# Attention head: the wait for the score banks behind seven projection steps, four steps after the first scores, three steps beside the first eleven units

## The chip, the core and the metric

The kernel runs on one core of a Trainium2 chip. The core has TensorE (matmuls, PE in the profile, its weight loads PEld), VectorE (DVE), ScalarE (ACT), GpSimd (POOL) and SyncE (SP, which issues DMAs only). The metric is device time in microseconds. TensorE writes its results to PSUM, which has eight banks of 128 x 512 floats; the other engines work on SBUF, and VectorE and ScalarE also read PSUM.

## What is computed

Two transformer blocks follow each other on 512 tokens of width 1024. The second has two layers, each with an attention, and the change lies in these two attentions. Cut to them:

```python
for layer in range(2):
    xn = rmsnorm(h, norm_mix[layer])
    if layer == 0:   # causal attention with a forget bias
        q, k, v, f_logit, qm = split(xn @ w_in_fox)
        mix = fox_attention(q, k, v, log_sigmoid(f_logit + b_forget))
    else:            # rotary positions, three dilated branches in one softmax by a mask
        q, k, v, qm = split(xn @ w_in_dil)
        mix = dilated_attention(apply_rope(q), apply_rope(k), v)
    mem_out = memory_attention(qm, rmsnorm(mem), w_mem_kv[layer])   # 256 memory tokens
    h = h + merge_heads(concat(mix, mem_out)) @ w_out[layer]        # 12 + 4 heads of 64
    h = h + conv_ffn(rmsnorm(h, norm_ffn[layer]), ...)
```

## The kernel before

Everything is float32. A projection tile ("piece") is 128 output columns by 512 tokens: eight blocks of 128 input features, each with three matmuls (high by high, high by low, low by high part), so 24 matmuls of 512 columns. `product_steps` (L1662) yields after every two blocks, so that a piece is four **steps** of six matmuls. GpSimd loads the weight pieces two ahead into four slots: the high part by DMA, its negation (L497), and the low part by an adding DMA (L500); it starts a piece when TensorE begins the one three places ahead of it.

`attention(layer, ready)` (L1799) works through 32 **units**: eight pairs of heads (two memory pairs, then six mixing pairs) by four blocks of 128 queries. The keys of a unit are 256 wide for a memory pair and 128, 256, 384, 512 for the blocks of a mixing pair. The projections q0, k0, v0, q1 ... v5 (`BESIDE_PIECES`, 18 pieces, 72 steps) run beside the units, and after them 14 short steps of the output projection (`head_block`, three matmuls each): 86 steps in all. TensorE's order is written out by hand: two steps, scores(0), four steps, and then for each unit u: scores(u+1), one step, possibly the transposes of a v piece, the transposes of unit u's probabilities (`turned`), the rest of `steps_of(u)`, and the output of unit u-1.

Between them the other engines do the softmax of a unit: VectorE adds the bias or mask and takes the maximum (`top_of`, L925, L927), ScalarE takes the exponents (L1602), VectorE divides (`divided`, L933, L935), TensorE transposes, ScalarE copies the transposed probabilities out of banks 4 and 5 (`kept`, L1610).

Banks: scores use 2 and 3, the beside pieces alternate between 0 and 1, and the pieces ahead of them (in layer 0 the forget piece, then memq0 and memq1) use 6, 7 and 2. Who empties a beside piece's bank: in layer 0 VectorE, for q and k with L862 and for v with L877; in layer 1 ScalarE for q and k (`rope_copy`, L1364), VectorE for v. In layer 1 a q or k piece is then rotated: SP moves its four strips into the shared tile `work[:, 4]` (four transfers, L475), and `rotated` on VectorE (L869 to L871) ends with the count `taken`. SP waits for the `taken` of one piece before it moves the next.

`done_at()` counts the steps and says in which unit a piece is complete (`DONE_AT`); from it all engines take when they evict (one unit later), take a v piece (two later) or rotate (three later).

```python
                for at in (2, 3):
                    pe.wait_ge(S(freed[at][0]), freed[at][1])
                if layer:
                    pe.wait_ge(S("mask_in"), 16)
                steps = beside()
                for _ in range(FIRST_STEPS[0]):
                    next(steps)
                scores(0)
```

Of the kernel before, what the change touches and what calls it, by code (L numbers as in the profile page):

```python
# [139 lines left out]
BESIDE_PIECES = [f"{name}{pair}" for pair in range(NP) for name in "qkv"]  # L140
FIRST_STEPS = (2, 4)


def steps_of(u):

    return 3 if u < 11 or u % 4 == 1 else 2

# [47 lines left out]
def build(nc, A, out):  # L195
# [17 lines left out]
    with ExitStack() as ctx:  # L213
# [303 lines left out]
        def _(dve):  # L517
# [321 lines left out]
            def vector_layer(layer):  # L839
# [97 lines left out]
                def beside(u):  # L937
# [3 lines left out]
                    for name, at in zip(BESIDE_PIECES, DONE_AT):  # L941
                        if u == at + taken_after(name, layer):
                            if name[0] == "v":
                                value_taken(name)
                            elif layer:
                                rotated(name)
                    for name, at in zip(BESIDE_PIECES, DONE_AT):
                        if u == at + 1:
                            if name[0] == "v":
# [5 lines left out]

                top_of(0)
                divided(0)
                for u in range(len(UNITS) + 2):
# [321 lines left out]
        def _(act):  # L1280
# [16 lines left out]
            def skip(tiles):  # L1297
                n.next("tile", tiles)
                n.value["bank"] += tiles
# [271 lines left out]
            for layer in range(2):  # L1571
# [33 lines left out]
                def kept(u):  # L1605
# [4 lines left out]
                    do(act.activation(at_m["pt"][:, u % 2, :, 0:width], banks8[:, 4:6, 0:width], ACT.Copy), "probs_kept")  # L1610

                exponents(0)
                for u in range(len(UNITS) + 2):
                    if u >= QB + 1 and (u - 1) % QB == 0:
                        pair_high(PAIRS[(u - 1) // QB - 1])
                    if u + 1 < len(UNITS):
                        exponents(u + 1)
                    for name, at in zip(BESIDE_PIECES, DONE_AT):
                        if u == at + 1:
                            if name[0] == "v" or layer == 0:  # L1620
                                skip(1)
                            else:
                                rope_copy(name)
                    if u < len(UNITS):
# [22 lines left out]
        def _(pe):  # L1647
# [151 lines left out]
            def attention(layer, ready):  # L1799
# [86 lines left out]
                def output(u):  # L1886
# [12 lines left out]
                    mm.then_inc(S("head_out"), 1)  # L1899

                for at in (2, 3):
                    pe.wait_ge(S(freed[at][0]), freed[at][1])
                if layer:
                    pe.wait_ge(S("mask_in"), 16)
                steps = beside()
                for _ in range(FIRST_STEPS[0]):
                    next(steps)
                scores(0)
# [402 lines left out]
```

## Time and profile before

| | us |
|---|---|
| median of three runs | 2222.05 |
| lowest and highest | 2220.85, 2223.23 |
| the profiled execution's own time | 2216.38 |
| its span in the trace | 2214.6 |
| TensorE busy in the span | 2099.2 (95%) |
| VectorE, GpSimd, ScalarE busy | 1290.1, 844.8, 466.4 |

The attention of layer 0 lies between about 983 and 1186 us, that of layer 1 between about 1597 and 1800 us. In the rows of a timeline a matmul's duration is modelled and overlaps the next one; the distance between the starts is its real cost in a stream. A bracket at the end of a row tells how long the engine sat idle before it and what released it.

### The profile page before, as it was taken

How to read it: one execution, taken by the hardware profiler on the slowest of the kernel's cores; microseconds unless marked ns; L12 is line 12 of the kernel's file. 1: busy time of each engine (PE TensorE's matmuls, PEld its weight loads, DVE VectorE, ACT ScalarE, POOL GpSimd, SP SyncE). 2: the span in 40 equal slices, each digit the busy share in tenths (PEclk: the TensorE clock that was granted, in tenths of full speed). 3: DMA queues.
4: the chain of work that ended last, by engine and by line, in shares of the span. 5: the costliest groups of instructions: out<-in, count | busy, mean ns of one | idle time of the engine just before them, and what ended most of it. 6: DMA issues, size and time to landing. Idle time of an engine off the chain costs nothing.

```text
span 2214.6 us, 27273 instructions
## 1 busy us (share of the span) xinstructions
PE 2099.2 (95%) x10722; PEld 1669.6 (75%) x10722; DVE 1290.1 (58%) x1798; ACT 466.4 (21%) x852; POOL 844.8 (38%) x1008
## 2 busy tenths in 40 slices
PE   6999898998899999989999999999899999999996
PEld 4778786676788888867777888888676678888885
DVE  7686664448662342574565763727546757637274
ACT  3013301213210000123333210202233432102011
POOL 1333323233444444433222444444422324444442
PEclk7999999999999999999999999999999999999998
DMA  8978776589998988866665889898776648899885
GB/s 285 206 176 190 146 144 143 115 222 244 247 237 187 194 194 196 191 147 153 128 138 132 189 181 203 192 193 181 173 152 133 131 110 188 189 198 193 193 188 123
DMA packets 124615, 394.40 MB, mean 178 GB/s; under 512 B 26028, under 2 KB 28076, under 8 KB 124232
## 3 DMA queue, kind: packets, MB, share of 16 engines
q0 software_dynamic: 96480, 346.20, 72.5%
q1 hardware_dynamic: 28008, 46.45, 6.6%
q8 instruction: 85, 1.39, 0.3%
q14 instruction: 42, 0.34, 0.0%
HBM read 385.63 MB, written 3.94 MB: 176 GB/s over the span
## 4 chain that ended last, share of the span: by engine, by line
PE 76%; DVE 13%; DMA 7%; issue 1%; ACT 1%; SPq 1%; POOL 1%; DVEq 0%; ACTq 0%
PE ps L1674 65%; DMA w_lo<-in_w 4%; PE ps L1703 2%; PE ps L1870 2%; PE ps L1897 1%; PE ps L1883 1%; DMA arena<-in_ada 1%; DMA w_hi<-in_w 1%; DVE work L754 1%; PE ps L2062 1%; DVE small L927 1%; DVE arena L755 1%; DVE arena L637 1%; DVE arena L925 1%; POOL w_lo L497 1%
## 5 line engine op out<-in xcount | busy, mean ns | idle before, releaser
L1674 PE MATMUL ps<-h_hi,w_hi 128*128 128x512 f32 x1760 | 710.9, 404 | 36.6 <-DVE arena L862 14.4
L1674 PE MATMUL ps<-h_lo,w_hi 128*128 128x512 f32 x1760 | 690.7, 392 | 0.0
L1674 PE MATMUL ps<-h_hi,w_lo 128*128 128x512 f32 x1760 | 690.6, 392 | 0.0
L491 POOL DMA_DIRECT2D w_hi<-in_w x334 | 186.6, 559 | 1166.8 <-PE ps L1674 1032.3
L1674 PEld LDWEIGHTS ps<-h_hi,w_hi 128*128 128x128 f32 x1760 | 333.4, 189 | 129.3 <-issue 25.1
L1674 PEld LDWEIGHTS ps<-h_hi,w_lo 128*128 128x128 f32 x1760 | 333.1, 189 | 71.6
L497 POOL TENSOR_SCALAR w_lo<-w_hi 128x1024 fp32r<-128x1024 f32 (+1 forms) x334 | 360.0, 1078 | 69.5 <-DMA w_hi<-in_w 64.0
L1674 PEld LDWEIGHTS ps<-h_lo,w_hi 128*128 128x128 f32 x1760 | 333.8, 190 | 65.7 <-issue 1.9
L500 POOL DMA_DIRECT2D w_lo<-in_w x334 | 300.5, 900 | 105.8 <-POOL w_lo L497 105.8
L1674 PE MATMUL ps<-g_hi,w_hi 128*128 128x512 f32 (+1 forms) x728 | 286.1, 393 | 8.4 <-DMA w_lo<-in_w 6.1
L1674 PE MATMUL ps<-g_lo,w_hi 128*128 128x512 f32 (+1 forms) x728 | 281.5, 387 | 0.0
L1674 PE MATMUL ps<-g_hi,w_lo 128*128 128x512 f32 (+1 forms) x728 | 281.4, 387 | 0.0
L1674 PEld LDWEIGHTS ps<-g_hi,w_hi 128*128 128x128 f32 x728 | 137.4, 189 | 42.8 <-DMA w_lo<-in_w 10.2
L1674 PEld LDWEIGHTS ps<-g_hi,w_lo 128*128 128x128 f32 x728 | 137.6, 189 | 27.9
L1674 PEld LDWEIGHTS ps<-g_lo,w_hi 128*128 128x128 f32 x728 | 137.7, 189 | 26.5 <-issue 0.2
L1638 ACT ACTIVATE arena<-arena,vec 128x512 f32<-128x512 f32 x88 | 71.8, 816 | 397.7 <-DVE arena L976 394.5
L987 DVE TENSOR_TENSOR x<-ps,x 128x512 f32<-128x512 f32 x48 | 33.2, 691 | 155.1 <-PE ps L1674 142.8
L981 DVE SCALAR_TENSOR_TENSOR arena<-arena,vec 128x511 f32<-128x511 f32 x88 | 114.4, 1300 | 3.1
L976 DVE TENSOR_TENSOR arena<-ps,work 128x512 f32<-128x512 f32 x88 | 60.8, 691 | 94.4 <-PE ps L1674 93.1
L1249 DVE TENSOR_TENSOR arena<-arena 128x512 f32<-128x512 f32 x32 | 52.4, 1638 | 82.8 <-ACT arena L1568 82.8
L1259 DVE SCALAR_TENSOR_TENSOR x<-ps,mod,x 128x512 f32<-128x512 f32 x32 | 24.0, 750 | 110.6 <-PE ps L1674 110.6
L1602 ACT ACTIVATE arena<-arena,small 128x128 f32<-128x128 f32 (+3 forms) x96 | 54.0, 563 | 151.7 <-DVE small L927 127.4
(376 smaller groups left out, 2134.4 us busy)
## 6 DMA issues: line engine op xcount, KB each, us to landing
w_hi<-in_w POOLq DMA_DIRECT2D x318, 512.0 KB, 3.9
w_lo<-in_w POOLq DMA_DIRECT2D x318, 512.0 KB, 5.6
arena<-in_ada SPq DMA_DIRECT2D x40, 512.0 KB, 8.2
w_hi<-in_w POOLq DMA_DIRECT2D x16, 384.0 KB, 3.3
w_lo<-in_w POOLq DMA_DIRECT2D x16, 384.0 KB, 5.0
x<-in_ada SPq DMA_DIRECT2D x8, 512.0 KB, 4.5
arena<-forget_sums SPq DMA_DIRECT2D x6, 512.0 KB
work<-arena SPq DMA_DIRECT2D x48, 64.0 KB, 3.3
```

The costliest lines, as they stand in the source:

```text
L491: pool.dma_start(w_hi[:, q % SLOTS, 0:n], A["w"][q][:, 0:n]).then_inc(S(f"high_in{q % SLOTS}"), 16)
L497: pool.tensor_scalar(w_lo[:, q % SLOTS, 0:n], w_hi[:, q % SLOTS, 0:n].bitcast(F32), -1.0, 0.0, ALU.mult, ALU.add).then_inc(S("negated"), 1)
L500: pool.dma_start(w_lo[:, q % SLOTS, 0:n], A["w"][q][:, 0:n], accum_op=ALU.add).then_inc(S(f"low_in{q % SLOTS}"), 16)
L976: do(dve.tensor_tensor(cv_m["z"][:, side, :], tile()[:], rstd, ALU.mult), "conv_scaled")
L981: do(dve.scalar_tensor_tensor(dst[:, 1:], z[:, :T - 1], w(1), dst[:, 1:], ALU.mult, ALU.add))
L987: update = lambda k: do(dve.tensor_tensor(x[:, k, :], tile()[:], x[:, k, :], ALU.add), "x_done")
L1249: do(dve.tensor_tensor(s, r, r, ALU.mult), "relu_used")
L1602: do(act.activation(pr, src, ACT.Exp, bias=row[:, g:g + 1], accum_out=row[:, 4 + g:5 + g]), "exped" if g else "act_step")
L1638: do(act.activation(c[:, j % 2, :], cv_m["z"][:, side, :], ACT.Identity, scale=V("cw2", at), bias=V("cb2", 44 * layer + 22 * side + j0 + j ...
L1674: mm = pe.matmul(bank, w[:, slot, cols], a(k), start=(k == 0 and i == 0), stop=(k == blocks - 1 and i == 2))
L1703: mm = pe.matmul(banks[i], w[:, slots[i], cols], a(k), start=(k == 0 and j == 0), stop=(k == blocks - 1 and j == 2))
L1870: mm = pe.matmul(ps[2 + g][:, 0:width], at_m["q"][half(g), pair, P * qb:P * qb + P], keys, start=True, stop=not fox)
```

## The change

`FIRST_STEPS` goes from (2, 4) to (7, 4): seven steps stand ahead of scores(0), and the waits for banks 2 and 3 and for the mask move behind them. `steps_of` gives three steps to the first eleven units and two to all others; before, every fourth unit after them (13, 17, 21, 25, 29) had three. The sum stays 86. Since k0 is now complete among the steps right after scores(0), the evictions are put in a function `evicted(done)` on VectorE and on ScalarE, which is also called once with -1 between the first unit's maximum (or exponents) and the next work.

```diff
-FIRST_STEPS = (2, 4)
+FIRST_STEPS = (7, 4)
...
-    return 3 if u < 11 or u % 4 == 1 else 2
+    return 3 if u < 11 else 2
...
+                    if u:
+                        evicted(u - 1)
+
+                def evicted(done):
+
                     for name, at in zip(BESIDE_PIECES, DONE_AT):
-                        if u == at + 1:
+                        if at == done:
                             if name[0] == "v":
                                 value_scaled(name)
...
                 top_of(0)
+                evicted(-1)
                 divided(0)
...
+                def evicted(done):
+                    for name, at in zip(BESIDE_PIECES, DONE_AT):
+                        if at == done:
+                            if name[0] == "v" or layer == 0:
+                                skip(1)
+                            else:
+                                rope_copy(name)
+
                 exponents(0)
+                evicted(-1)
...
-                    for name, at in zip(BESIDE_PIECES, DONE_AT):
-                        if u == at + 1:
-                            if name[0] == "v" or layer == 0:
-                                skip(1)
-                            else:
-                                rope_copy(name)
+                    if u:
+                        evicted(u - 1)
...
+                steps = beside()
+                for _ in range(FIRST_STEPS[0]):
+                    next(steps)
                 for at in (2, 3):
                     pe.wait_ge(S(freed[at][0]), freed[at][1])
                 if layer:
                     pe.wait_ge(S("mask_in"), 16)
-                steps = beside()
-                for _ in range(FIRST_STEPS[0]):
-                    next(steps)
                 scores(0)
```

The unit in which each piece is complete, before and after (-1 is ahead of unit 0): q0 -1, -1; k0 0, -1; v0 1, 0; q1 3, 1; k1 4, 2; v1 5, 4; q2 7, 5; k2 8, 6; v2 9, 8; q3 11, 9; k3 13, 10; v3 14, 12; q4 16, 14; k4 18, 16; v4 20, 18; q5 21, 20; k5 23, 22; v5 25, 24.

TensorE at the start of layer 1's attention, before: h_hi and h_lo are the projections' operands, the first row is q0's first matmul, and L1870 is scores(0).

```order
L1674 MATMUL ps<-h_hi,w_hi 128x512 [waits low_in0,mask_in,x_done,dve_freed]
L1674 MATMUL ps<-h_lo,w_hi 128x512
L1674 MATMUL ps<-h_hi,w_lo 128x512
...
L1870 MATMUL ps<-arena 128x256 [waits dve_freed,mem_scaled]
L1870 MATMUL ps<-arena 128x256
```

After, the same place (scores are L1881 there, the projections L1685); the row with `rope_copied` is v0's first matmul.

```order
L1685 MATMUL ps<-h_hi,w_hi 128x512 [waits x_done,low_in0]
L1685 MATMUL ps<-h_lo,w_hi 128x512
...
L1881 MATMUL ps<-arena 128x256 [waits mem_scaled,mask_in,dve_freed,x_done]
L1881 MATMUL ps<-arena 128x256
...
L1685 MATMUL ps<-h_hi,w_hi 128x512 [waits rope_copied,low_in2]
L1685 MATMUL ps<-h_lo,w_hi 128x512
```

The waits for `mask_in` and for the banks moved from q0's first matmul to scores(0), and v0's first matmul, six matmuls behind scores(0), now waits for `rope_copied`, ScalarE's copy of q0.

ScalarE at the same place, before: L1602 are the exponents of units 0 and 1, L1364 the copy of q0.

```order
L1602 ACT_TABLE_LOAD [waits scores_read]
L1602 ACTIVATE arena,small<-ps,small 128x256 [waits rms_ready]
L1602 ACTIVATE arena,small<-ps,small 128x256 [waits act_step]
L1602 ACTIVATE arena,small<-ps,small 128x256 [waits scores_read,exped]
L1602 ACTIVATE arena,small<-ps,small 128x256 [waits act_step]
L1364 ACTIVATE arena<-ps 128x512 [waits tile,exped]
```

After (exponents are L1608, copies L1370):

```order
L1608 ACT_TABLE_LOAD [waits scores_read]
L1608 ACTIVATE arena,small<-ps,small 128x256 [waits rms_ready]
L1608 ACTIVATE arena,small<-ps,small 128x256 [waits act_step]
L1370 ACTIVATE arena<-ps 128x512 [waits tile,exped]
L1370 ACTIVATE arena<-ps 128x512 [waits tile,rope_copied]
L1608 ACTIVATE arena,small<-ps,small 128x256 [waits scores_read,rope_copied]
```

The copies of q0 and k0 now stand together between the exponents of unit 0 and of unit 1.

VectorE in layer 1 from unit 2's call of `top_of(3)`, before: the rotation of q0, v0's scaling, the division of unit 3.

```order
L927 TENSOR_REDUCE small<-ps 128x2 [waits scores,probs]
L869 TENSOR_TENSOR work<-work 128x512 [waits rope_in,scores_read]
L870 TENSOR_TENSOR arena<-arena,work 128x512 [waits dve_step]
L871 TENSOR_TENSOR arena<-arena,work 128x512 [waits dve_step]
L877 TENSOR_TENSOR arena<-ps,work 128x512 [waits tile,taken]
L933 RECIPROCAL small<-small 128x2 [waits exped,v_scaled]
```

After:

```order
L927 TENSOR_REDUCE small<-ps 128x2 [waits scores,probs]
L869 TENSOR_TENSOR work<-work 128x512 [waits rope_in,scores_read]
L870 TENSOR_TENSOR arena<-arena,work 128x512 [waits dve_step]
L871 TENSOR_TENSOR arena<-arena,work 128x512 [waits dve_step]
L869 TENSOR_TENSOR work<-work 128x512 [waits rope_in,taken]
L870 TENSOR_TENSOR arena<-arena,work 128x512 [waits dve_step]
L871 TENSOR_TENSOR arena<-arena,work 128x512 [waits dve_step]
L883 COPY arena<-ps 128x4x128 [waits turned,taken]
L933 RECIPROCAL small<-small 128x2 [waits exped,taken]
```

Two rotations and the copy of v0 now stand between the maximum and the division of unit 3; before, k0's rotation stood a unit later.

## Rows read from the trace of the kernel before

**Rows 1.** the page: busy time by engine, and the chain that ended last

```profile
PE 2099.2 (95%) x10722; PEld 1669.6 (75%) x10722; DVE 1290.1 (58%) x1798; ACT 466.4 (21%) x852; POOL 844.8 (38%) x1008
...
PE 76%; DVE 13%; DMA 7%; issue 1%; ACT 1%; SPq 1%; POOL 1%; DVEq 0%; ACTq 0%
```

**Rows 2.** timeline, TensorE, layer 0: start us, us, engine, line, instruction [idle before]

```profile
980.15 0.39 PE L1674 MATMUL ps<-h_hi,w_hi 128*128 128x512 f32 x1
...
983.32 0.39 PE L1674 MATMUL ps<-h_hi,w_lo 128*128 128x512 f32 x1
992.93 0.79 PE L1674 MATMUL ps<-h_hi,w_hi 128*128 128x512 f32 x1 [9.22 <-DVE arena L862]
...
997.38 0.70 PE L1870 MATMUL ps<-arena 64*128 64x256 f32 x4
```

**Rows 3.** timeline, VectorE, layer 0, ahead of the first scores

```profile
990.75 0.68 DVE L890 TENSOR_TENSOR work<-work 12x512 f32<-12x512 f32 x1
991.46 1.42 DVE L862 SCALAR_TENSOR_TENSOR arena<-ps,work 128x512 f32<-128x512 f32 x2
```

**Rows 4.** timeline, TensorE, head of layer 1

```profile
1597.50 0.39 PE L1674 MATMUL ps<-h_hi,w_lo 128*128 128x512 f32 x1
1603.10 0.80 PE L1674 MATMUL ps<-h_hi,w_hi 128*128 128x512 f32 x1 [5.21 <-DVE arena L862]
...
1607.93 0.70 PE L1870 MATMUL ps<-arena 64*128 64x256 f32 x4
```

**Rows 5.** stretches: busy us of PE, PEld, DVE, ACT, POOL; then granted clock, DMA share, GB/s

```profile
543.00:547.00 4.00, 3.61 (x16) 2.98 (x17) 3.79 (x7) 0.20 (x1) 1.52 (x2) 1.00 1.08 356
...
590.00:594.00 4.00, 3.13 (x16) 2.84 (x16) 0.00 (x0) 1.66 (x3) 1.67 (x2) 0.58 1.00 232
...
993.00:996.00 3.00, 3.00 (x7) 2.41 (x8) 0.00 (x0) 2.34 (x3) 1.65 (x3) 0.50 0.28 61
...
1774.00:1777.00 3.00, 3.00 (x15) 2.84 (x14) 2.35 (x7) 1.29 (x5) 0.00 (x0) 0.57 0.57 112
```

**Rows 6.** timeline, TensorE, layer 1: two starts of scores, and three waits

```profile
1625.64 0.70 PE L1870 MATMUL ps<-arena 64*128 64x256 f32 x4
...
1631.65 0.70 PE L1870 MATMUL ps<-arena 64*128 64x256 f32 x4
...
1643.44 0.47 PE L1674 MATMUL ps<-h_hi,w_hi 128*128 128x512 f32 x1 [0.86 <-ACT arena L1364]
...
1669.84 0.47 PE L1674 MATMUL ps<-h_hi,w_hi 128*128 128x512 f32 x1 [1.76 <-ACT arena L1364]
...
1772.83 0.49 PE L1870 MATMUL ps<-arena 64*128 64x128 f32 x4 [2.72 <-DVE arena L871]
```

**Rows 7.** timeline, VectorE, layer 1: rotations (L869 to L871) and a wide unit

```profile
1627.19 2.07 DVE L869 TENSOR_TENSOR work<-work 128x512 f32<-128x512 f32 x1
...
1630.02 0.69 DVE L871 TENSOR_TENSOR arena<-arena,work 128x512 f32<-128x512 f32 x1
...
1636.31 1.23 DVE L869 TENSOR_TENSOR work<-work 128x512 f32<-128x512 f32 x1 [3.14 <-DMA work<-arena]
...
1680.52 1.22 DVE L927 TENSOR_REDUCE small<-arena 128x2 f32<-128x1024 f32 x1
```

**Rows 8.** timeline, ScalarE, layer 1: first exponents, and a copy of a q piece

```profile
1609.55 1.28 ACT L1602 ACT_TABLE_LOAD   x1 [16.33 <-DVE small L927]
...
1611.82 0.19 ACT L1602 ACTIVATION_READ_ACCUMULATOR arena<-ps,small 128x1 f32 x1
...
1642.70 0.60 ACT L1364 ACTIVATE arena<-ps 128x512 f32<-128x512 f32 x1
```

**Rows 9.** timeline, GpSimd, layer 1: a negation

```profile
1627.64 1.06 POOL L497 TENSOR_SCALAR w_lo<-w_hi 128x1024 fp32r<-128x1024 f32 x1
```

**Rows 10.** timeline, TensorE, layer 0, near its last unit

```profile
1179.21 1.06 PE L1883 MATMUL ps<-con,arena 128*128 128x128 f32 x8 [1.73 <-ACT arena L1610]
```

**Rows 11.** DMAs of the strips in layer 1 (tile work)

```profile
DMA to landing us min/median/max: 2.0/3.3/5.3
```

## The prediction

> **What bounds the kernel now.** I read the page first [rows 1]: TensorE is busy 95% of the span and carries 76% of the chain that ended last, so what counts is what TensorE waits for and how fast it is clocked. Next, TensorE's timeline at the head of each attention. In layer 0 the last matmul of memq1 starts at 983.32 and the next one at 992.93, released by VectorE at L862 [rows 2]: 9.22 us idle, because the wait for score banks 2 and 3 stands ahead of all projection steps and VectorE frees bank 2 only with its last L862 (two of them, 991.46 + 1.42 = 992.88) [rows 3]. In layer 1 the same gap is 5.21 us, 1597.50 to 1603.10 [rows 4]. After such a gap the granted clock is 0.50 [rows 5], the lower level, 1.2 GHz: twelve matmuls up to the first scores take 4.45 us in layer 0 (992.93 to 997.38) and 4.83 in layer 1, where twelve at 2.4 GHz take 12 x 0.227 = 2.7 us (the spacing ahead of the gap: 14 matmuls between 980.15 and 983.32 [rows 2]). Third, the waits inside layer 1's attention [rows 6], and fourth VectorE and ScalarE there [rows 7, 8], since they set when TensorE's banks come free.
>
> **Part 1, the wait behind seven steps (removed idle).** A step is six matmuls, seven steps are 42, 42 x 0.227 = 9.5 us. Layer 0: they run from 983.55, so scores(0) can start at 993.1. Banks are freed at 992.88, with one addition: the weight piece triggered by the second beside piece, at 989.0, brings GpSimd's negation (L497) to about 990.7, 1.7 us after it, and L890 stands there [rows 3]. In layer 1 an L869 that met a negation took 2.07 us in place of 0.69 [rows 7, 9]. I add 1.0, so 993.9. Before, scores(0) stood at 997.38 with 12 matmuls done; now at 993.9 with 42: 3.5 + 30 x 0.227 = **10.3 us gained** (11.0 if the negation misses). Layer 1: 1597.73 + 9.5 = 1607.2 against 1607.93, VectorE is done at 1603.05, so 0.6 + 6.8 = **7.4 us gained**. Weights hide this: pieces land at the pace that the projections ahead of the gap use.
>
> The GPSIMD Engine Reference of the Trainium skill (section Specifications) says that GpSimd shares its SBUF interfaces with VectorE and contends with instructions that read two SBUF inputs; L890 and L869 do, L862 reads PSUM. By the rule both additions stand; were it void the sum below would be 1.9 us lower.
>
> **Part 2, a new wait at the head of layer 1.** Piece v0 begins one step after scores(0) and takes q0's bank. In layer 1 ScalarE empties it, and now `evicted(-1)` stands behind exponents(0). From the rows, counted from the start of scores(0) at 1607.93: table load at 1.62, last accumulator read ends at 4.08, copy 0.60 more [rows 8], so 4.84 with the release; TensorE is ready at 0.63 + 1.49 = 2.12. **2.7 us lost.** In layer 0 VectorE empties q0 right after its reduction: 2.36 against 2.12, 0.25 us. k0's eviction and divided(0) hide behind the exponent there.
>
> **Part 3, the rotations of layer 1.** Each q or k piece goes ScalarE, four 64 KB transfers on SP's queue, VectorE (L869 to L871). SP issues k's transfers only after q's L871, since they share one tile: 1630.71 to 1636.31 is 5.6 us [rows 7]; for the next two pairs I found 5.17 and 4.77, so 5.2. Now q0 and k0 finish together, and both rotations fall in unit 2 (before in units 2 and 3). Counted from the start of scores(3): reduction over at 1.5, q0 rotated at 3.7 (3 x 0.72), k0's strips at 8.9, rotated at 11.1, v0's copy 11.8, first probabilities 12.9 with release. TensorE wants them after a unit of three steps with v0's turn (6.0 [rows 6] + 0.43), scores(4) 0.63 and a step 1.49: 8.6. Stall 4.3, with v1's negation falling on k0's rotation 5.1. That is near the 5.21 us gap of rows 4, after which twelve matmuls cost about 2 us more, so I add 1.7 for the clock. Before, this pair cost 1.5 (0.86 idle before L1674 [rows 6] and its surroundings). **+5.3.**
>
> Second pair, now units 4 and 5: k1's strips come 2.9 us into unit 5, rotated 5.1, v1's scaling 5.8, which TensorE's third step wants at 4.0: 1.9 us, against 2.3 before (1.76 idle [rows 6], 0.28, 0.25). **-0.4.** Third pair, units 8 and 9: reduction, pair_low and rotation of k2 end at 6.0 to 7.1, v2 scaled 0.7 later, wanted at 4.2: 2.6 to 3.7, take 3.1, plus 1.6 for the clock, less 1.3 before. **+3.4.** Fourth pair, units 12 and 13 (before 14 and 16, no wait on this path): unit 13 has the add and reduction of 384 columns, pair_low, the rotation and v3's scaling, 8.8 us on VectorE until probabilities(14), wanted at 7.2; unit 14 with 512 columns (2.5 for add and reduction, each as the 1.22 of [rows 7], and the exponents) runs 1.0 late again. 2.7, and 0.6 in units 17 to 19. **+3.3.**
>
> **The clock in short stalls.** Idles of 2.0 to 2.8 us are followed by a stretch at half rate in four of five places: 590 to 594 at 0.58 and 1774 to 1777 at 0.57, after L1870 waited 2.72 [rows 5, 6]; 543 to 547 kept 1.00 [rows 5]. Such a stretch costs some 1.6 us. Shorter idles (1.73 in [rows 10], 1.76) show none. For Part 2 I take 0.8 x 1.6 = **1.3 us**.
>
> **Part 4, one step fewer at every fourth unit after 11.** Matmuls are neither added nor lost: both orders issue 86 steps. Two steps are done one unit earlier, so in unit 25 TensorE has two short steps of three matmuls where two full ones and a short one stood. VectorE then sets the pace. Layer 0: units 25 to 27 took 15.1 us, less 2.15 of moved work 13.0; now 14.0 by VectorE's chain (add and reduction, exponents, division), 15.3 if a negation meets L935. **+1.3.** Two banks in layer 0 come back 0.2 and 0.35 late (v0, v2). Layer 1: k5's rotation, one unit earlier, no longer holds scores(28), where 2.72 us went [rows 6]; yet v5's turn and the next two probabilities come 1.5 and 2.0 late, 17.75 against 17.73 us. **0.**
>
> **Sum:** -10.3 - 7.4 + 2.7 + 1.3 + 0.25 + 5.3 - 0.4 + 3.4 + 3.3 + 1.3 + 0.55 = 0.0 us. Against the profiled execution (2216.4 us, span 2214.6) nothing, so I forecast the median, 2222.0; that execution stands 5.7 us under the median, more than any term here but two, and the differences are put on the median.
>
> **The rivals.** (a) *The gain at the heads survives.* Strips in 4.8 us rather than 5.2, no negation on a critical instruction, no half clock after stalls under 5 us: 0.4 x 3 pairs + 2.2 (1.0 and 0.8 for the two negations, 0.4 in the third pair) + 4.6 (1.7, 1.6 and 1.3 of clock) = 8.0 less, 2214. For it: 2.20 us did not drop the clock [rows 5]. Against: four of five did.
> (b) *Slower.* One mechanism: in layer 1 VectorE is the serial path from unit 2 to 19. If a late probability pushes the next unit's add and reduction, the stall comes again one unit later, as I grant it only in unit 14; once more in units 3, 6 and 10 at 1.0 to 2.0 us each, and the half clock behind one of them, +6, 2228. It decides where a unit's VectorE work (up to 6.6 us) exceeds TensorE's 6.0 or, after unit 11, 4.6 to 5.3. Against: units 3 to 10 have three full steps, 0.3 to 2 us of slack.
> (c) *The idle moves rather than goes.* If the second beside piece's low half landed late, the seven steps would wait for weights, as elsewhere before L1674. The piece ahead was triggered 11 us earlier and transfers take 3.9 and 5.6 us, so little speaks for it: +2 in each layer, 2226.
>
> By the page DMA: Bandwidth & Descriptors of the Trainium skill (section Issuing engines are not separate DMA queues), transfers issued by any engine run on the same 16 engines and interleave, so an unbroken stream of weights would slow the strips; they land in 2.0 to 5.3 us, median 3.3 [rows 11]. With the slowest for two pairs the sum would be +4, still within no change.
>
> **How the numbers follow.** 0.2% (4.4 us) is about what a measurement of this kernel can tell from no change. Cancellation within it 0.48, (c) included with 0.04; (a) and milder forms 0.32; (b) 0.20. Eight in ten times: from 2214, where the three discounts of (a) all come, to 2228, where (b) is full. The likeliest case alone: 2218 to 2226.
>
> **What would show it.** Right: no idle before the first beside matmul and clock 1.00 at both heads; 1 us or less before scores(0) in layer 0 and none in layer 1; in layer 1 a wait of 2.7 us on ScalarE's copy one step after scores(0), then 4 to 5 us on L935's counterpart in unit 3 with half clock behind it, about 2 in unit 5, 3 in unit 9, 2 in unit 14; nothing new in layer 0 before unit 25. Wrong: layer 1's attention as long as before or shorter means that Part 3 was oversized, and the time is (a)'s.

## The result, and the profile after

The changed kernel takes **2226.82 us** (median of 20 runs, 2220.83 to 2233.41), the kernel before 2221.81 us (20 runs, 2216.5 to 2225.89) beside it. The ratio is **1.002, with a 95% interval of 1.0011 to 1.0028**: slower by 4.4 us by the ratio and 5.0 by the medians. That is about the 0.2% that the prediction called no change, but it is clear of zero, and it is neither the prediction's sum (2222) nor its rival (a) (2214). In size it stands with rival (c) (2226) and rival (b) (2228); whether the mechanism of either is at work is looked at below.

The page after, its span and its busy line, stands against [rows 1]:

```profile
span 2231.0 us, 27273 instructions
...
PE 2105.8 (94%) x10722; PEld 1672.6 (75%) x10722; DVE 1287.5 (58%) x1798; ACT 466.3 (21%) x852; POOL 842.2 (38%) x1008
```

The span is 16.4 us above that of before, three times what the medians differ by. To see which part belongs to the change, a fixed instruction is needed on either side of each attention. Four transposes of TensorE serve (they write `ps` from `work` and `con`): one ahead of the attention of layer 0, one behind it, and the same in layer 1. TensorE's timeline, before and then after:

```profile
970.91 1.88 PE L1763 MATMUL ps<-work,con 128*128 128x512 f32 x4
1225.24 1.02 PE L1763 MATMUL ps<-work,con 128*128 128x512 f32 x2
1591.42 1.02 PE L1763 MATMUL ps<-work,con 128*128 128x512 f32 x2
1838.60 1.02 PE L1763 MATMUL ps<-work,con 128*128 128x512 f32 x2
```

```profile
975.86 1.88 PE L1774 MATMUL ps<-work,con 128*128 128x512 f32 x4
1225.43 1.02 PE L1774 MATMUL ps<-work,con 128*128 128x512 f32 x2
1591.17 1.02 PE L1774 MATMUL ps<-work,con 128*128 128x512 f32 x2
1852.02 1.02 PE L1774 MATMUL ps<-work,con 128*128 128x512 f32 x2
```

Layer 0's stretch goes from 254.33 to 249.57 us (-4.8), the stretch between the layers stays (366.18 and 365.74), layer 1's goes from 247.18 to **260.85 us (+13.7)**. The first row already stands 4.95 us later, though nothing ahead of it was changed: in the 13 traces of this study that row (or its first part) lies anywhere from 967.29 to 979.21. So about 7.5 of the 16.4 us are not the change's. From here on every trace is read by these two stretches.

How well does a stretch repeat? Each trace is one execution. The new order of layer 0 stands in ten of the traces, with stretches from 246.70 to 249.57 us (the changed kernel's own is the longest), the old one in two, 254.33 and 254.62. Layer 1's stretch was 247.18 and 246.04 us in the old order and 260.85 and 260.98 in the new one. Taken from scores(0) to scores(31) alone, the two traces of either order of layer 1 agree within 0.9 us. So a difference of 3 us or more between two stretches can be read, and one of 1 to 2 us can't be read by itself.

**The heads came as forecast.** In layer 0 TensorE runs unbroken up to scores(0), and waits 1.12 us there; the granted clock is 1.00 from 984.0 to 999.2 and, in layer 1, from 1590 to 1607, where scores(0) doesn't wait at all. With no wait for weights among the seven steps, rival (c) falls. In layer 0 VectorE is late by L888, an instruction of 12 x 512 that overlapped GpSimd's negation and took 1.77 us in place of 0.47. TensorE, then VectorE before and after, then GpSimd after:

```profile
999.30 0.70 PE L1881 MATMUL ps<-arena 64*128 64x256 f32 x4 [1.12 <-DVE arena L862]
```

```profile
989.79 0.47 DVE L888 TENSOR_SCALAR work<-work,vec 12x512 f32<-12x512 f32 x1
```

```profile
994.77 1.77 DVE L888 TENSOR_SCALAR work<-work,vec 12x512 f32<-12x512 f32 x1
```

```profile
995.19 1.07 POOL L497 TENSOR_SCALAR w_lo<-w_hi 128x1024 fp32r<-128x1024 f32 x1
```

scores(0) stands 23.44 us behind the first transposes (26.47 before), with five more steps done (five steps of six matmuls are 6.8 us): 3.0 + 6.8 = 9.8 us gained, against 10.3. In layer 1 it is 15.93 against 16.51, 0.6 + 6.8 = 7.4 gained, as forecast.

**Layer 1's loop lost more.** The longest entries in the list of TensorE's waits from scores(0) to scores(31) there, after (engine, line, what it waited for; us in total, times, longest):

```profile
PE ps L1685 <- DVE arena L877: 8.6, 2, 4.7
PE ps L1894 <- DVE arena L935: 5.6, 3, 3.4
PE ps L1685 <- ACT arena L1370: 2.6, 1, 2.6
```

The four long ones, in TensorE's timeline, and the granted clock of the 4 us behind each (the eighth value of a row, after the busy times):

```profile
1611.94 0.77 PE L1685 MATMUL ps<-h_hi,w_hi 128*128 128x512 f32 x1 [2.56 <-ACT arena L1370]
...
1641.13 0.83 PE L1894 MATMUL ps<-con,arena 128*128 128x128 f32 x4 [3.42 <-DVE arena L935]
...
1660.83 0.77 PE L1685 MATMUL ps<-h_hi,w_hi 128*128 128x512 f32 x1 [3.88 <-DVE arena L877]
...
1692.34 0.77 PE L1685 MATMUL ps<-h_hi,w_hi 128*128 128x512 f32 x1 [4.71 <-DVE arena L877]
```

```profile
1612.00:1616.00 4.00, 4.00 (x12) 3.21 (x13) 0.21 (x1) 0.42 (x1) 2.48 (x3) 0.64 0.47 126
1641.00:1645.00 4.00, 3.87 (x13) 2.96 (x14) 1.99 (x6) 2.32 (x6) 0.00 (x0) 0.64 0.80 174
1661.00:1665.00 4.00, 4.00 (x16) 2.63 (x18) 0.62 (x2) 0.00 (x0) 2.51 (x3) 0.50 0.46 120
1692.00:1696.00 4.00, 3.67 (x12) 2.33 (x14) 1.19 (x4) 0.00 (x0) 2.27 (x3) 0.50 0.35 77
```

They stand in units 0 (one step after scores(0)), 3, 5 and 9, where Parts 2 and 3 of the prediction put them, but two are larger: 3.88 where 1.9 was forecast, 4.71 where 3.1 was. Behind each the granted clock is 0.50 to 0.64. VectorE in front of the third one shows the reason: k1's rotation (L869 to L871) sits idle for its strips, and v1's scaling (L877), which frees TensorE's bank, stands behind it:

```profile
1649.81 0.69 DVE L871 TENSOR_TENSOR arena<-arena,work 128x512 f32<-128x512 f32 x1
...
1657.81 0.69 DVE L869 TENSOR_TENSOR work<-work 128x512 f32<-128x512 f32 x1 [2.75 <-DMA work<-arena]
1658.54 0.69 DVE L870 TENSOR_TENSOR arena<-arena,work 128x512 f32<-128x512 f32 x1
1659.26 0.69 DVE L871 TENSOR_TENSOR arena<-arena,work 128x512 f32<-128x512 f32 x1
1659.99 0.69 DVE L877 TENSOR_TENSOR arena<-ps,work 128x512 f32<-128x512 f32 x1
```

The list of waits gives L877 as the cause; L877 stands behind the rotation, so the time was lost at the strips. The strips were released at 1650.50 (end of q1's L871) and read at 1657.81, **7.3 us** later; the prediction took 5.2. For k2 it is 6.6 (1682.74 to 1689.32), for k0 4.0 (1632.68 to 1636.69).

### The profile page after: what moved, and what is told of

The parts are those of the page before. It is cut to its first block, busy times and chain, and to the rows that moved or that the text cites. A ratio compares the mean times of both kernels' runs of the same rounds, so it can differ in the third digit from the quotient of the medians.

```text
span 2231.0 us, 27273 instructions
## 1 busy us (share of the span) xinstructions
PE 2105.8 (94%) x10722; PEld 1672.6 (75%) x10722; DVE 1287.5 (58%) x1798; ACT 466.3 (21%) x852; POOL 842.2 (38%) x1008
## 4 chain that ended last, share of the span: by engine, by line
PE 75%; DVE 13%; DMA 8%; issue 2%; ACT 1%; SPq 1%; POOL 1%; DVEq 0%; ACTq 0%
PE ps L1685 63%; DMA w_lo<-in_w 4%; PE ps L1714 2%; DMA w_hi<-in_w 2%; PE ps L1881 2%; PE ps L1908 2%; PE ps L1894 1%; DMA arena<-in_ada 1%; DVE work L754 1%; DVE small L927 1%; PE ps L2073 1%; DVE arena L925 1%; DVE arena L755 1%; POOL w_lo L497 1%; DVE arena L637 1%
## 5 line engine op out<-in xcount | busy, mean ns | idle before, releaser
L1685 PE MATMUL ps<-h_hi,w_hi 128*128 128x512 f32 x1760 | 712.0, 405 | 36.3 <-DMA w_lo<-in_w 12.2
L1685 PE MATMUL ps<-h_hi,w_lo 128*128 128x512 f32 x1760 | 692.6, 394 | 0.0
L1685 PE MATMUL ps<-h_lo,w_hi 128*128 128x512 f32 x1760 | 691.7, 393 | 0.0
L1685 PEld LDWEIGHTS ps<-h_hi,w_hi 128*128 128x128 f32 x1760 | 334.1, 190 | 130.1 <-issue 35.1
L1685 PEld LDWEIGHTS ps<-h_hi,w_lo 128*128 128x128 f32 x1760 | 333.6, 190 | 71.5
L1685 PEld LDWEIGHTS ps<-h_lo,w_hi 128*128 128x128 f32 x1760 | 334.7, 190 | 66.2 <-issue 1.9
L1685 PE MATMUL ps<-g_hi,w_hi 128*128 128x512 f32 (+1 forms) x728 | 286.3, 393 | 9.6 <-DMA w_lo<-in_w 7.6
L1685 PE MATMUL ps<-g_hi,w_lo 128*128 128x512 f32 (+1 forms) x728 | 282.7, 388 | 0.0
L1685 PE MATMUL ps<-g_lo,w_hi 128*128 128x512 f32 (+1 forms) x728 | 282.4, 388 | 0.0
L1685 PEld LDWEIGHTS ps<-g_hi,w_hi 128*128 128x128 f32 x728 | 138.3, 190 | 43.2 <-DMA w_lo<-in_w 11.0
L1685 PEld LDWEIGHTS ps<-g_hi,w_lo 128*128 128x128 f32 x728 | 138.3, 190 | 27.8
L1685 PEld LDWEIGHTS ps<-g_lo,w_hi 128*128 128x128 f32 x728 | 138.3, 190 | 26.7 <-issue 0.2
L1608 ACT ACTIVATE arena<-arena,small 128x128 f32<-128x128 f32 (+3 forms) x96 | 54.0, 563 | 147.8 <-DVE small L927 129.1
```

Of the source, the lines that this page charges most:

```text
L1608: do(act.activation(pr, src, ACT.Exp, bias=row[:, g:g + 1], accum_out=row[:, 4 + g:5 + g]), "exped" if g else "act_step")
L1685: mm = pe.matmul(bank, w[:, slot, cols], a(k), start=(k == 0 and i == 0), stop=(k == blocks - 1 and i == 2))
```

## The experiments

**1. One layer at a time.** `FIRST_STEPS`, `steps_of` and `DONE_AT` get a value for each layer; the other layer keeps the old order.

```
-    return 3 if u < 11 else 2
+    return 3 if u < 11 or (u % 4 == 1 and not NEW[layer]) else 2
...
-                    if u:
+                    if u or not NEW[layer]:
                         evicted(u - 1)
```

> The change is made in the attention of layer 0 alone; layer 1 keeps the old order (two steps behind the wait, three steps also at every fourth unit). The prediction's terms for layer 0 (-10.3 + 0.25 + 1.3 + 0.55) say -8.2 us, 2213.6. The trace of the changed kernel says -9.8 at the head, +3.5 in the loop and +1.5 in a slowly clocked stretch behind it, -4.8 us, 2217. Rival: the head's gain is a shift that is lost again before the layer ends, no change (2222). In the trace: no idle before the first beside matmul, scores(0) about 3 us earlier than before, counted from memq1, with five more steps done.

> The change is made in the attention of layer 1 alone; layer 0 keeps the old order. The prediction's terms for layer 1 (-7.4 + 4.0 + 5.3 - 0.4 + 3.4 + 3.3) say +8.2 us, 2230. The trace of the changed kernel says -7.4 at the head and +21 us of new waits and slow clock in the loop, +13.7, 2235.5. Since the whole change costs 5 us, this run and the one with layer 0 alone should add up to +5: -8.2 with +13 or -4.8 with +10. Rival: each layer alone costs about 2.5 us, so that nothing is tied to the rotations (2224).

Measured: layer 0 alone 2210.74 us, ratio 0.9958 (0.9941 to 0.9974), -9.3 us; layer 1 alone 2235.51 us, ratio 1.0065 (1.0047 to 1.0082), +14.4. The sum is +5.1, what the whole change costs (either interval is some 3.8 us wide to each side). Layer 0 gains and layer 1 loses, and no sign shows that the layers act on each other. In the traces layer 0's stretch is 246.81 us with the change alone in layer 0 (254.33 before), layer 1's is 260.98 with it alone in layer 1 (260.85 in the changed kernel). That each layer costs about 2.5 us, the rival written down for this run, falls.

**2. Two tiles for the strips.** Does k's rotation wait for the release by q's, or for the transfer?

```
+        STRIPS = (work[:, 4, :], room[:])
...
-                if r:
-                    sp.wait_ge(S("taken"), TURNED_BASE[1] + TURNED[1].index(ROPED[r - 1]) + 1)
+                if r > 1:
+                    sp.wait_ge(S("taken"), TURNED_BASE[1] + TURNED[1].index(ROPED[r - 2]) + 1)
...
-                    t, u = turn_room(1, i), work[:, 4, :]
+                    t, u = turn_room(1, i), STRIPS[ROPED.index(name) % 2]
```

The strips of either tile are counted on a semaphore of their own.

> The changed kernel with two tiles for the strips of a rotation, used in turn, so that the four transfers of k0 (k1, ...) no longer wait for the last instruction of q0's rotation (q1's, ...). If that release is what makes units 3, 5 and 9 of layer 1 late, VectorE's waits for strips (4.0, 2.8 and about 6 us) go, TensorE's waits of 3.4, 3.9 and 4.7 us shrink to 1 us or less, and two or three stretches of half clock (1.6 us each) go with them: 8 to 14 us less than the changed kernel, 2213 to 2219. Rival one, the transfers are late because weights fill the queues, whatever releases them: VectorE still waits over 2 us at the same places and the time stays within 3 us of the changed kernel, 2224 to 2228. Rival two, VectorE's serial work is too long even without the waits: TensorE's waits fall by 1 us each only, 2222.

Measured: **2213.52 us**, ratio 0.9969 (0.9958 to 0.9981), 13 us under the changed kernel. Layer 1's stretch is 248.82 (260.85). VectorE waits for no strips any more; of TensorE's waits the one in unit 3 is gone and those in units 5 and 9 are 1.16 and 2.40:

```profile
PE ps L1686 <- DVE arena L878: 3.6, 2, 2.4
PE ps L1686 <- ACT arena L1371: 2.6, 1, 2.6
PE ps L1895 <- DVE arena L936: 2.2, 2, 1.1
```

So some 12 of the 13.7 us that layer 1 lost hang on VectorE's idle time ahead of k's rotation. (Unit 0 was 1.4 us shorter here and unit 27 1.4 us longer, places with no wait for strips; the two cancel.) The rival that VectorE's serial work is too long by itself falls for most of it; what it leaves is the 1.2, the 2.4 and the two 1.1.

**3. Thin weights.** Why did k1's and k2's strips take 7.3 and 6.6 us, and k0's 4.0? DMA share and GB/s (the last two values) around k1's, after:

```profile
1650.00:1651.00 1.00, 1.00 (x6) 0.79 (x5) 0.93 (x3) 0.23 (x1) 0.91 (x2) 1.00 0.00 0
1651.00:1654.00 3.00, 3.00 (x20) 1.96 (x19) 1.57 (x3) 0.60 (x1) 1.60 (x2) 1.00 1.01 224
1654.00:1658.00 4.00, 2.95 (x15) 2.08 (x13) 1.22 (x3) 1.73 (x5) 0.00 (x0) 1.00 0.86 159
```

The DMA engines stand still until 1651 and are then full for 3 us and 86% busy for 4 more: GpSimd triggers the high half of a weight piece (512 KB) 0.4 us ahead of the strips' release at 1650.50, and the low half (512 KB) 1.5 us behind it:

```profile
1650.08 0.55 POOL L491 DMA_DIRECT2D w_hi<-in_w  x1 [10.40 <-PE ps L1685]
...
1652.01 0.89 POOL L500 DMA_DIRECT2D w_lo<-in_w  x1 [0.30 <-POOL w_lo L497]
```

```
+            def sent(q, n):
+                return 16 if first_thin <= q < first_thin + len(BESIDE_PIECES) else n
-                pool.dma_start(w_hi[:, q % SLOTS, 0:n], A["w"][q][:, 0:n])...
+                pool.dma_start(w_hi[:, q % SLOTS, 0:sent(q, n)], A["w"][q][:, 0:sent(q, n)])...
```

> The changed kernel, but the weight pieces of layer 1's attention are sent with 16 of their 1024 columns (both halves; GpSimd's negation stays whole), so that hardly any weight traffic runs beside the strips; the projections there compute with stale weights. If the strips of k1 and k2 landed 7.3 and 6.6 us after VectorE's last L871 because a weight piece was triggered just before them, they now land within 4.7 us, as k0's did, in every pair; VectorE's waits for them fall from 2.75 and 2.35 us to under 0.5, TensorE's waits in units 5 and 9 from 3.9 and 4.7 us to about 1.3 and 2.5, and layer 1's attention is 5 to 7 us shorter. If the hand-over from VectorE to SP and the four issues set the time, nothing falls by more than 0.5 us and layer 1's attention stays as long as in the changed kernel (260.9 us from the transposes ahead of it to those behind). Unit 3 tells nothing apart, it should keep 3 us or more in either case.

Measured (one profiled run, 2223.41 us): layer 1's stretch **252.80 us** (260.85), 8.05 less, where 5 to 7 were expected. VectorE waits once more for strips, for k0's, and as long as before (4.0); k1's strips are there 4.6 us after the release or sooner, since their rotation follows the instruction ahead of it without a gap, and TensorE's waits in units 5 and 9 are exactly those that two tiles left. Unit by unit, units 5, 6, 9 and 10 are 9.4 us shorter together, while unit 3 is 1.0 us longer behind the same idle. VectorE, then TensorE:

```profile
1635.75 0.69 DVE L875 TENSOR_TENSOR work<-work 128x512 f32<-128x512 f32 x1 [4.01 <-DMA work<-arena]
...
1654.42 0.69 DVE L916 TENSOR_TENSOR g_lo<-ps,g_hi 128x512 fp32r<-128x512 f32 x1
1655.15 0.69 DVE L875 TENSOR_TENSOR work<-work 128x512 f32<-128x512 f32 x1
```

```profile
1640.18 1.11 PE L1900 MATMUL ps<-con,arena 128*128 128x128 f32 x4 [3.41 <-DVE arena L941]
...
1658.16 0.47 PE L1691 MATMUL ps<-h_hi,w_hi 128*128 128x512 f32 x1 [1.16 <-DVE arena L883]
...
1685.03 0.47 PE L1691 MATMUL ps<-h_hi,w_hi 128*128 128x512 f32 x1 [2.40 <-DVE arena L883]
```

The two causes are now apart: hand-over, issue and transfer alone take 4.0 us (k0, without weight traffic), the weight piece adds the rest in the second and third pair. That it is the bytes and not GpSimd's work is shown by this run, since GpSimd's instructions are all still there. A full set of DMA engines is not enough by itself, though: in the changed kernel k0's strips, released at 1632.68, ran beside the rest of a half piece that had been triggered 3.1 us ahead (its row, and the share of 1.03 in the first 1.3 us) and took 4.0 us as well:

```profile
1629.58 0.89 POOL L500 DMA_DIRECT2D w_lo<-in_w  x1 [0.30 <-POOL w_lo L497]
```

```profile
1632.00:1634.00 2.00, 2.00 (x11) 1.68 (x10) 0.68 (x1) 0.98 (x2) 0.00 (x0) 1.00 1.03 188
```

What tells the pairs apart is the time between the trigger of the low half and the release of the strips (the end of L871). The traces of before and after have six pairs in which VectorE waited for strips, and they fall in one order:

| trace, piece | low half triggered | release to first use, us |
|---|---|---|
| after, k0 | 3.1 us ahead | 4.0 |
| before, k2 | 2.1 us ahead | 4.8 |
| before, k1 | 1.7 us ahead | 5.2 |
| before, k0 | 1.4 us ahead | 5.6 |
| after, k2 | 0.25 us ahead | 6.6 |
| after, k1 | 1.5 us behind (high half 0.4 ahead) | 7.3 |

The same pairs in four other traces without a second tile lie between 3.95 and 7.4 us in the same order. The triggers of the low half, three before and the one for k2 after, and the end of k2's wait after:

```profile
1629.31 0.89 POOL L500 DMA_DIRECT2D w_lo<-in_w  x1 [0.60 <-POOL w_lo L497]
...
1654.96 0.90 POOL L500 DMA_DIRECT2D w_lo<-in_w  x1 [0.30 <-POOL w_lo L497]
...
1681.83 0.89 POOL L500 DMA_DIRECT2D w_lo<-in_w  x1 [0.30 <-POOL w_lo L497]
```

```profile
1682.49 0.92 POOL L500 DMA_DIRECT2D w_lo<-in_w  x1 [0.30 <-POOL w_lo L497]
```

```profile
1689.32 0.69 DVE L869 TENSOR_TENSOR work<-work 128x512 f32<-128x512 f32 x1 [2.35 <-DMA work<-arena]
```

This is an order found in traces, not one made by an edit: the thin weights show that the bytes are the cause, but no run moves a trigger and keeps its bytes.

**4. q0's copy ahead of the first exponents** in layer 1, on ScalarE:

```
+                if layer:
+                    evicted(-1)
                 exponents(0)
-                evicted(-1)
+                if layer == 0:
+                    evicted(-1)
```

(The strips are counted on another semaphore as well.)

> The changed kernel with ScalarE's copy of q0 ahead of the first exponents in layer 1 (bank 0 is done before the first scores). TensorE's wait of 2.56 us ahead of v0's first matmul should go, and the half clock behind it (1.6 us) with it: 4.2 us less than the changed kernel, 2222.6. Rival: without that idle the next wait, in unit 3, grows by as much, since VectorE's strips there don't come earlier: no gain, or 1.6 of clock alone, 2225 to 2227.

Measured: 2222.60 us, ratio 1.0003 (0.999 to 1.0015), 4.2 us under the changed kernel; layer 1's stretch 257.00, 3.85 less. The wait of 2.56 is gone and unit 0 takes 6.32 us in place of 10.47, the wait in unit 3 is still 3.42. The price of Part 2 (2.7 + 1.3) was right for the changed kernel, and it is not paid back later.

**5. Both edits, and rotations last.** First experiments 2 and 4 together; then also VectorE's rotations and copies of turned values at the end of a unit in layer 1 (`if layer: all_taken(u)` behind `divided(u + 1)`).

> The changed kernel with both edits, two tiles for the strips and q0's copy ahead of the first exponents in layer 1. They take away different waits, so the gains should add: 13.3 + 4.2 us less than the changed kernel's 2226.8, 2209.5. Rival: after the head the copies only shift VectorE's work, and the remaining waits on v1's and v2's scaling (1.2 and 2.4 us) grow by as much: 2213, as with two strips alone.

> As the run before, and in layer 1 VectorE does the rotations and the copies of turned values at the end of a unit, behind the division and behind the scaling of v. If the waits that are left in units 5 and 9 (1.2 and 2.4 us on v's scaling) come only from VectorE's order within a unit, they go too, with the clock behind them: 4 to 6 us less than the run before, 2204 to 2206. Rival: the rotation then holds up the next unit's add and reduction, and the waits come back one unit later on the probabilities (L935): no gain, 2209 to 2211.

Measured: 2211.40 us, ratio 0.9951 (0.9935 to 0.9967), and 2210.64 us, 0.995 (0.9935 to 0.9965). The stretches are 245.23 and 243.57 us. 248.82 less 3.85 would be 245.0, so the two edits add, as far as single stretches tell. Neither the whole times nor the stretches, 1.7 us apart, tell the two kernels safely apart; the last edit brings 1.7 at most where 4 to 6 were expected: of the waits in units 5 and 9 one of 0.86 is left, but near the end of the loop stand two that the run before did not have, 0.66 and 1.48 us, and one of 2.54 in place of 2.03. The rival (no gain) was right in size, and waits come back, only later in the loop.

**6. The old order in layer 1, with two tiles.** The change in layer 0 as in experiment 1, the strips as in experiment 2.

> The change in layer 0 alone, layer 1 in the old order, but with two tiles for the strips. The old order waits 3.1, 2.6 and 1.9 us on VectorE for strips and TensorE 0.9, 1.8, 1.1 and 2.9 us behind the rotations; if the second tile removes them, 3 to 6 us less than layer 0 alone gave (2210.7), 2205 to 2208, about as good as the new order in both layers with both edits: then the seven steps in layer 1 bring only what they take. Rival: in the old order the strips hide already, no gain, 2210.7.

Measured: 2211.33 us, ratio 0.9951 (0.9934 to 0.9967), no less than layer 0 alone, and the spread of six runs (2208.28 to 2219.73) is wider than the effect looked for. The stretch is clearer: 241.61 us against 246.04 in the run with layer 0 alone, both in the old order. Against the new order with the same two tiles (248.82) it is 7.2 us less, though 4 us of idle still stand at its head; against the new order with all three edits (243.57) it is 2.0 less, which single stretches don't settle. So with two tiles alone seven steps in layer 1 are still worse than two, in the stretch; the whole times (2213.52 and 2211.33) lean the same way but their intervals overlap.

**7. Four steps instead of seven in layer 1.**

```
-FIRST_STEPS = (7, 4)
+FIRST_STEPS = ((7, 4), (4, 3))
...
-    return 3 if u < 11 else 2
+    return 3 if u < 11 or (layer and u % 4 == 1) else 2
```

Against the changed kernel this alters three numbers of layer 1 at once (seven to four, four to three, and the third steps come back). Against the old order it alters only the steps around scores(0), from two and four to four and three.

> Layer 0 as in the changed kernel; in layer 1 four steps stand ahead of the wait for the banks and three behind the first scores, and the three steps at every fourth unit are kept. The idle there was 5.2 us and four steps are 24 x 0.227 = 5.4, so the head should still gain the full 7.4 us, while the rotations of q and k fall two units apart (units 2 and 3, 5 and 7, 9 and 11). If the loss of the changed kernel comes from rotations that fall in one unit or in neighbours, layer 1's attention takes 240 to 242 us between the transposes (247.2 before, 260.9 with seven), and the time is 2203 to 2206. Rival: any step taken ahead at the head is paid back by VectorE's path in the loop, layer 1 stays at 246 or more, 2210.

> The run before with two tiles for the strips. In the old order the second tile took 4.4 us off layer 1's attention (246.0 to 241.6); if it does so here, 236 to 238 us and 2199 to 2202. Rival: with rotations two units apart the strips of k have time to land anyway, 240 us, no gain.

Measured: **2206.39 us, ratio 0.9928 (0.9909 to 0.9947)**, 15 us under the kernel before and 20 under the changed one; with two tiles 2204.67, ratio 0.9923 (0.9906 to 0.9939). The two intervals overlap almost wholly, and in the traces the second tile brings nothing (236.99 and 237.84 us), so its rival held. With four steps the stretch is 10 us under the old order's 247.18 and 9 under its 246.04, and 3 us under the 240 to 242 expected. Layer 1's stretch with four steps:

```profile
1583.75 1.02 PE L1774 MATMUL ps<-work,con 128*128 128x512 f32 x2
...
1595.59 0.70 PE L1881 MATMUL ps<-arena 64*128 64x256 f32 x4
...
1820.74 1.02 PE L1774 MATMUL ps<-work,con 128*128 128x512 f32 x2
```

scores(0) stands 11.84 us behind the transposes, exactly three steps (3 x 1.36) less than with seven: no idle either (with two tiles scores(0) waited 1.00 us in its one trace). The head's whole gain is there, and in the loop the waits of units 0, 3, 5 and 9 are gone, but for 0.9 us in unit 9:

```profile
PE ps L1881 <- DVE arena L871: 2.2, 1, 2.2
...
PE ps L1807 <- DVE arena L877: 1.2, 1, 1.2
PE ps L1685 <- ACT arena L1370: 0.9, 1, 0.9
```

**8. The third steps put back.** The changed kernel with the old `steps_of`.

> The changed kernel with the third step at every fourth unit after 11 put back, so that of the change only the seven steps and the early evictions are left. By Part 4 of the prediction (the third steps taken away cost 1.3 us in layer 0 and nothing in layer 1) putting them back should give 1.3 us. Against it: with eleven steps ahead of unit 0 and the old units the steps run out about three units earlier, so units 23 to 27 stand without projections and VectorE sets their pace; then layer 0's attention takes 2 to 4 us longer than in the changed kernel (247 to 249.6 between the transposes) and the waits of 1.1 us in units 14 to 19 of layer 1 go, 1 to 2 us less there.

Measured (one profiled run, 2240.78 us): layer 0's stretch 254.53 us (249.57), layer 1's 264.58 (260.85). In layer 1 the waits of 1.1 us are one of 0.5, as expected, but at the end TensorE waits 2.96 and 3.92 us for VectorE and ScalarE with nothing left to project. The expectation that was drawn from Part 4 fell. The one against it held for layer 0, where it was too small; in layer 1, where it looked for 1 to 2 us less, the stretch is 3.7 us longer. Once eleven steps stand ahead of unit 0, taking the third steps away saves 5.0 us or more in layer 0 (against the other nine traces of the new order 5.4 to 7.8) and 3.7 in layer 1. Note what that means for layer 0: with seven steps ahead and the old `steps_of` its stretch is as long as before the change (254.53 against 254.33). The 9.8 us gained at the head stay only because both edits were made together.

## Why the prediction missed

The prediction had Part 1, Part 2 and the places of the stalls right. The step that failed is a term of Part 3: the 5.2 us that the strips of k were given from the release by q's L871 to their first use. They measured 7.3 us for k1 and 6.6 for k2. The sums below are made of the times from one scores to the next, after less before.

- **Part 1, heads (-10.3, -7.4):** measured -9.8 and -7.4. Right; the negation fell on L888 rather than L890 and cost 1.3, not 1.0.
- **Part 2 (+2.7, +1.3):** idle 2.56, unit 0 longer by 4.2 in all; taking it away gave 3.85. Right, but the clock's share was not certain: with two tiles the same idle cost 2.8 in all.
- **Part 3, first pair (+5.3):** unit by unit +0.41 + 4.97 - 1.50 = +3.9. Smaller, mostly since strips came 4.0 us after the release, not 5.2.
- **Part 3, second pair (-0.4):** measured +5.88 + 0.99 - 0.47 - 2.35 = **+4.05**. Here the failed term weighs most: the 5.2 us from one L871 to the next L869 was the mean of three pairs of the old order (5.60 of them in [rows 7]), in which the low half of a weight piece had been triggered 1.4 to 2.1 us ahead. It was carried to places where the piece falls right beside the release; it was 7.3. With 5.2 the idle was 1.9, below the 2.0 from which I charged for the clock; with 7.3 it was 3.88 and the clock behind it fell to 0.50, which together cost 5.9 in one unit.
- **Part 3, third pair (+3.4):** measured **+6.15**, the same term (6.6 for 5.2), idle 4.71 for 3.1, clock 0.50.
- **Part 3, fourth pair and units 17 to 19 (+3.3):** two waits of 1.1 us, in units 15 and 19, +2.3 in all. The wait of 2.7 in unit 14 did not come.
- **Part 4, layer 1 (0), and layer 0's loop (+1.3 + 0.55, with +0.25 from Part 2):** +0.6, and in layer 0's loop +3.5 after, +2.7 in the run of layer 0 alone. A little low, and credited to the wrong edit: taking the third steps away saves (experiment 8), the cost belongs to the five steps that were moved ahead.
- **In the working:** the negation at layer 0's head is worth 0.7 by Part 1 (11.0 against 10.3) but 1.0 in rival (a), and the two negations make 1.8 us, not 1.9. Neither slip moves the sum.

For layer 1 the terms made +8.2 and the trace shows +13.7: -1.4 and +4.45 and +2.75 from the three pairs, -1.0 from the fourth, and 0.7 from unit 0, Part 4 and the end. Luck kept the miss small: the second and third pairs were 7.2 us too low, the first and fourth 2.4 too high. For layer 0 they made -8.2; the trace of the changed kernel shows -4.8, that of layer 0 alone -7.5, the timing of it -9.3, so within what one stretch can tell that sum was about right. Part of what the changed kernel's trace gained less is clock: the wait of 1.73 us at L1894 is the same in both, yet 0.58 stands behind it in the one and 1.00 in the other, in that order:

```profile
1178.00:1182.00 4.00, 4.00 (x27) 3.25 (x28) 0.18 (x1) 1.02 (x1) 0.00 (x0) 0.58 0.00 0
```

```profile
1171.00:1175.00 4.00, 3.30 (x39) 2.64 (x38) 0.18 (x1) 1.62 (x2) 0.00 (x0) 1.00 0.00 0
```

Rival (b) named a time near the measured one (2228) and the right place, VectorE in layer 1, by another mechanism: it put new stalls in units 3, 6 and 10 through VectorE's own work. No wait over 0.1 us stands in units 6 and 10. VectorE was idle, not busy, in front of the stalls that grew. Rival (c) (2226) had the nearest time and a mechanism that did not happen: TensorE waited for no weights at either head. The prediction had the true mechanism in its working, in the sentence that with the slowest landings "the sum would be +4", and called that still no change; with the clock behind the longer stalls it was worth more. The trace bears out that sentence's source, the Trainium skill, DMA: Bandwidth & Descriptors, section Issuing engines are not separate DMA queues: transfers from SP and GpSimd shared the engines, 7.3 us for k1's strips against 4.6 or less without the weights.

Open: no run shifted a weight piece against the strips with its bytes kept, so the table of experiment 3 is an order seen, not a rule tested. Nor does a run take seven steps down to four with `steps_of` as in the changed kernel.

## What to carry to other kernels

Size the work that is put ahead of a wait by the idle time it has to fill. Here four steps for an idle of 5.2 us kept the head's whole gain, and seven kept no more of it; the three surplus steps went with two rotations in one unit and a layer 1 stretch 24 us longer (`steps_of` differs between those two kernels as well, so the step count is not shown to be the whole of it). Then look at what the moved work leaves at the other end: in layer 0 seven steps gained nothing over the stretch until the step plan of the late units was changed too.

When a transfer's latency enters a sum, don't carry over its mean. Look up, for each place of the new order, what other transfers are triggered around its release; the slow landings here had one between 2.1 us ahead and 1.5 us behind. The three values behind the mean, 5.6, 5.2 and 4.8, already followed that distance in the trace of before.

And compare traces by a pair of fixed instructions around the stage, with the same pair taken in several traces of unchanged code to learn how far it repeats.

## What the runs showed of the hardware

- Four transfers of 64 KB between places in SBUF took, from release to first use, 4.0 us without weight traffic and 7.3 us when a piece of 512 KB and its other half were triggered 0.4 us ahead and 1.5 us behind; in between, the nearer the second half's trigger, the longer (the table of experiment 3).
- GpSimd's negation slowed a VectorE instruction with a single tensor input too: L888, 12 x 512, took 1.77 us in place of 0.47. The prediction had looked for it at instructions with two SBUF inputs alone. The line of the Trainium skill that it went by (GPSIMD Engine Reference, section Specifications) also names instructions in a 2-port perf mode, which the prediction left out. No row here shows in which mode L888 ran, so the row neither contradicts the page nor proves it.
- The clock behind a short stall is not fixed by the stall. Behind the same 2.56 us of idle, at the same matmul, it was 0.63 to 0.66 over 4 us in four traces, the changed kernel's among them, and 1.00 with two tiles. Unit 0 took 10.47 to 10.74 us there and 9.10 with two tiles, against 6.32 without the idle: 2.56 us of idle cost 2.8 to 4.4. Behind 1.72 to 1.73 us in layer 0 it was 0.58 and 1.00. Behind all three idles of 3.4 us and more in the changed kernel's loop it was 0.64 or 0.50.

```profile
1607.00:1611.00 4.00, 4.00 (x21) 3.03 (x19) 0.00 (x0) 0.00 (x0) 2.51 (x3) 1.00 0.72 165
```

(The stretch behind the 2.56 us of idle, with two tiles.)
